# V gathers four places further behind the U gathers in a hybrid mixer and expert-gather kernel

## The reference

```python
q = (xt @ w_query).reshape(T, Hh, 2, PEER_HALF)          # 128 tokens, 8 heads
s = jnp.einsum('thpc,pnc->thpn', q, sub_keys)
sv, si = lax.top_k(s, K)                                 # 16 of 128, twice
fv, fi = lax.top_k(cand, K)                              # 16 of the 256 pair sums
eidx = jnp.take_along_axis(cidx, fi, axis=-1)
g = jax.nn.softmax(fv, axis=-1)
ue, ve = expert_u[eidx], expert_v[eidx]                  # rows of 1024 from 16384 experts
act = jax.nn.gelu(jnp.einsum('td,thkd->thk', xt, ue), approximate=False)
return jnp.einsum('thk,thkd->td', (g * act), ve)
```

## Time and profile before

| | us |
|---|---|
| median of 3 runs | 3545.51 |
| lowest, highest | 3544.26, 3552.44 |
| the profiled execution | 3540.44 |
| its span, first to last instruction | 3538.7 |
| mean granted TensorE clock | 0.765 of full |

### The profile page before, as it was taken

One profiled execution on the slowest core, in us unless ns is written; L12 is line 12 of the kernel. 1 busy time (PEld: TensorE's weight loads), 2 busy tenths in 40 slices (PEclk: granted clock), 3 DMA queues, 4 the chain that ended last, 5 costly groups with the idle time before them and its releaser, 6 DMA issues.

```text
span 3538.7 us, 32708 instructions
## 1 busy us (share of the span) xinstructions
PE 2224.0 (63%) x10776; PEld 1135.5 (32%) x10776; DVE 2182.0 (62%) x5516; ACT 628.7 (18%) x1358; POOL 1941.3 (55%) x2079
## 2 busy tenths in 40 slices
PE   8999986545665466546764478456664577444433
PEld 6767762212322133213421233123321343111110
DVE  4544357765766676666676676657666666665753
ACT  1221132111221022102211132113310232100000
POOL 0000026666666666666666666666466655666665
PEclk9999997776777677767776788677876787766655
DMA  5211369999999999999999999999899999999998
GB/s 193 67 41 38 114 243 360 378 382 361 363 357 392 370 370 343 384 378 360 387 369 376 358 368 354 386 371 349 305 370 377 360 336 346 364 370 377 368 366 325
DMA packets 337953, 1156.72 MB, mean 327 GB/s; under 512 B 36404, under 2 KB 50424, under 8 KB 336760
## 3 DMA queue, kind: packets, MB, share of 16 engines
q0 software_dynamic: 294912, 1073.87, 79.7%
q1 hardware_dynamic: 42872, 80.75, 6.6%
HBM read 1136.64 MB, written 17.84 MB: 326 GB/s over the span
## 4 chain that ended last, share of the span: by engine, by line
PE 30%; POOL 24%; issue 17%; DVE 11%; another core or an unknown queue 10%; DMA 6%; ACT 2%; POOLq 0%; DVEq 0%; ACTq 0%
POOL work L705 12%; POOL work L688 12%; PE xs L1516 10%; PE xs_ahead L1516 8%; PE acc L1516 7%; DVE work L1398 5%; PE bank L1516 4%; DMA work<-expert_u,chosen 4%; DMA work<-expert_v,idx_v 2%; DVE work L1024 1%; DVE cand L1016 1%; DVE rest L1298 0%; DVE work L1016 0%; ACT work L859 0%
## 5 line engine op out<-in xcount | busy, mean ns | idle before, releaser
L1398 DVE CUSTOM_DVE_ANT_0 work<-work,xs 128x1024 f32<-128x1024 f32 x1003 | 1210.7, 1218 | 527.2 <-DMA work<-expert_u,chosen 296.6
L688 POOL DMA_INDIRECT work<-expert_u,chosen x1024 | 966.7, 944 | 859.2 <-DVE chosen L1024 469.6
L705 POOL DMA_INDIRECT work<-expert_v,idx_v x1024 | 969.6, 947 | 720.8 <-remote 316.2
L1516 PE MATMUL acc<-work,lw 128*32 128x512 f32 x4096 | 822.9, 865 | 578.6 <-DMA work<-expert_v,idx_v 303.2
L1516 PEld LDWEIGHTS acc<-work,lw 128*32 128x32 f32 x4096 | 148.2, 138 | 1013.3 <-issue 589.6
L1516 PE MATMUL bank<-weights,n2T 128*128 128x256 f32 x1024 | 255.4, 405 | 0.0
L1516 PEld LDWEIGHTS bank<-weights,n2T 128*128 128x128 f32 x1024 | 203.2, 205 | 110.9 <-issue 84.0
L1516 PE MATMUL bank<-which_eight,c_spread 128*128 128x16 f32 x128 | 35.6, 357 | 309.3 <-issue 143.4
L1516 PE MATMUL xs_ahead<-work,neg_tri 128*128 128x512 f32 (+1 forms) x176 | 130.9, 835 | 129.5 <-DVE work L1024 72.6
L1516 PE MATMUL xs<-work,weights 128*128 128x128 f32 x1664 | 195.4, 280 | 0.0
L1516 PEld LDWEIGHTS xs<-work,weights 128*128 128x128 f32 x1664 | 191.7, 195 | 1.4 <-issue 1.3
(11 more groups left out here) (203 smaller groups left out, 2414.2 us busy)
## 6 DMA issues: line engine op xcount, KB each, us to landing
work<-kv_dram SPq DMA_DIRECT2D x72, 256.0 KB
work<-expert_u,chosen POOLq DMA_INDIRECT x1024
work<-expert_v,idx_v POOLq DMA_INDIRECT x1024
weights<-w_in SPq DMA_DIRECT2D x6, 2048.0 KB, 17.6
mix_dram<-work SPq DMA_DIRECT2D x8, 1024.0 KB, 4.1
weights<-w_queryT SPq DMA_DIRECT2D x4, 2048.0 KB, 7.8
work<-xT SPq DMA_DIRECT2D x9, 512.0 KB, 7.2
kv_dram<-work SPq DMA_DIRECT2D x9, 512.0 KB, 5.9
```

The lines of the kernel that those rows point to most:

```text
L688: pool.indirect_dma_start(out=ring_u[:, s, :], out_offset=None, in_=expert_u, in_offset=bass.IndirectOffsetOnAxis(ap=chosen[:, G % KEPT_HE ...
L705: pool.indirect_dma_start(out=ring_v[:, e % RING_V, :], out_offset=None, in_=expert_v, in_offset=bass.IndirectOffsetOnAxis(ap=idx_v[:, G % ...
L1398: nc.vector.tensor_tensor_reduce(s, s, rows[:, :, :].rearrange("p a b -> p (a b)"), 1.0, 0.0, ALU.mult, ALU.add, dots[:, d:d + 1]).then_in ...
L1516: return nc.tensor.matmul(out_, lhsT, rhs, start=start, stop=stop, skip_group_check=True)
```

## The change

POOL's loop runs over single places instead of heads, and the V gather is the one 20 places (`BEHIND = TOPK + SET`) behind the U gather instead of 16. A head's first V gather is issued with the fifth U gather of the next head instead of the first; at the end 20 V gathers follow the last U gather instead of 16. All other engines' programs, `V_LAG`, both rings and every semaphore value stay.

```diff
+BEHIND = TOPK + SET
...
-            for G in range(HEADS + 1):
+            for n in range(HEADS * TOPK + BEHIND):
+                G, k = divmod(n, TOPK)
                 if G < HEADS:
-                    pool.wait_ge(idx_ready, G + 1)
-                if G > 0:
-                    pool.wait_ge(idx_v_ready, G)
-                for k in range(TOPK):
-                    if G < HEADS:
-                        gather_u(G, k)
-                    if G > 0:
-                        gather_v(G - 1, k)
+                    if k == 0:
+                        pool.wait_ge(idx_ready, G + 1)
+                    gather_u(G, k)
+                G, k = divmod(n - BEHIND, TOPK)
+                if G >= 0:
+                    if k == 0:
+                        pool.wait_ge(idx_v_ready, G + 1)
+                    gather_v(G, k)
```

## The result

The changed kernel takes **3672.61 us** (3665.81 to 3676.30, four runs) against 3544.89 us (3538.02 to 3552.44, four runs) of the kernel before on the same chip: a ratio of **1.0362, 95% interval 1.0332 to 1.0391**, 128 us slower. Forecast were 3580 us and at most 3665 us. The direction was right, the size a bit over a quarter of what came.

A forecast was written before the change was run, and what follows sets the result against it. DMA transfers at nine tenths looked like the bound, with POOL standing about 500 us, 404 us of it before V gathers. Terms 6.6 - 26 + 48 + 6 = +35 us gave 3580 us, 1.0% slower; range 3480 to 3665 us.

The forecast's parts named there:

- (a): Start and end of POOL's gather stream: 20 instead of 16 V gathers after the last U gather, +6.6 us.
- (b): POOL's V gathers waiting for PE: half of 44 stops' recoverable time saved, -26 us, bounds 0 and -123 us.
- held signals: PE's sum done, but word reaches waiting engines late (11.6 us in one head); 119 "remote" V stops, 316.2 us, assumed unchanged.
- (c): PE's scores and mixing queued behind later V sums, delaying DVE: 2 us in 24 heads, +48 us, bounds 0 and +106.
- the cover: U ring's slack before a late dot stops POOL's U gather: 12.5 us in a light head, 1.5 us in a loaded one.
- the prediction's own last sign of being wrong: POOL waiting for dots in heads without mixing would show that the U ring's slack was not there.
- (d): DVE's residual add at place 17 waits for PE's set of place 16: +6 us in all, bounds 0 and 35 us.
- PE's lateness was the bound: Rival, chance 0.28: all 44 V stops for PE vanish and the kernel ends faster, 3435 us, or likelier 3500 us.
- the coupling takes the mixing too: Rival, chance 0.12: z, s and av also late behind PE's sums, 4.4 us in 42 heads; 3737 us, half 3645 us.
- The ends alone: Rival, chance 0.17: transfers fill their engines, stops are only exchanged, nothing but the ends moves; 3545 to 3553 us.

The follow-up runs named there:

- e1: Changed kernel with PE's sums of V sets and the residual add four places later (V_LAG 6): 3602.91 us, 1.0126 to the kernel before.
- e13: The changed kernel, unaltered, on a chip where PE's signals are prompt: 3292.59 us against 3260.93 us for the kernel before, 1.0102.
- e3: Changed kernel with the scores issued on PE ahead of the set's sum at place 4: 3633.10 us, 1.0198 to the kernel before.
- e6: Kernel before with the scores issued on PE ahead of the set's sum at place 4: 3561.68 us, 1.0036.
- e7: Changed kernel; ahead of each U gather POOL also waits for the landing of the one two places earlier: 3845.31 us, 1.0829.
- e9: Changed kernel with at most five gathers in flight (a wait ahead of each V gather), on a chip with prompt signals: 3421.53 us, 1.0491.
- e16: Kernel before with at most five gathers in flight (a wait ahead of each V gather), on a chip with prompt signals: 3406.91 us, 1.0454.
- e12: Kernel before with eight U and nine V buffers instead of 7 and 10, on a chip with prompt signals: 3269.88 us, 1.0024.

## Why the forecast was right in sign and short in size

(a) *The ends* held. The first U gather came at 479.1 us, 3.9 us later than before, which e1 and e13 with the same start don't show (475.7 and 474.9 us) and e3 does (479.0 us), so it belongs to the execution; from the last U gather to the last V gather POOL took 3655.43 - 3624.64 = 30.8 us against 26.3, so +4.4 us for a forecast of 6.6:

```profile
3624.64 0.94 POOL L689 DMA_INDIRECT work<-expert_u,chosen  x1 [0.31 <-issue]
...
3655.43 0.93 POOL L706 DMA_INDIRECT work<-expert_v,idx_v  x1 [0.30 <-issue]
```

(b) *The V gates* were taken at -26 us, with the held signals left where they were. That half failed in fact: the remote stops halved, 316 to 167 us, outside the 60 us given. They lie before the third V gather of a set, and if PE is late or DVE stops the U gathers first, POOL isn't there in time to be stopped. The stops for PE fell to 24.8 us as expected. That the saving would be given back by the U ring was the right idea.

(c) *The coupling* was the right mechanism and the mis-sized term. Three of its parts were measured. The push of the scores was 6.8 us in the head opened above, for 5.6 worked out in a loaded one. In heads without mixing the cover did hold where I had looked: in the sixth head of tile 8 DVE now stands 9.20 us for the scores, more than the 4.6 forecast, and no U gather of that head stops.

```profile
3526.31 4.19 PE L1518 MATMUL bank<-weights,n2T 128*128 128x256 f32 x16
```
```profile
3530.54 0.50 DVE L1296 MAX8 srt<-bank 128x8 f32<-128x128 f32 x2 [9.20 <-PE bank L1518]
```

But in the last three heads of tiles 2 to 7 the U gathers stand 53 us in all where they had stood for none, and in the second head of tile 8, which has no mixing, they stand 12 us (7 behind DVE's wait for scores, 5 behind its wait for the residual add): a cover read off one head was taken for all. That is the prediction's own last sign of being wrong. The step that failed is the sentence that a held signal makes the push cost 0 and that 4.4 us is its upper end. In the second heads, where the signal had mostly been prompt, it is now late by 8 to 11 us, on top of the push; 62 us come from these six heads, against 12 in the sum (2 us each) and 26 at the upper bound. The 24 heads for which the sum had 48 us, at most 106, became 6 x 17.9 = 107 us longer, and that with the saving of (b) already in it. The push also reached DVE by two ways that the sum had at nothing, `weigh` and the mixing: +63 and +91 us of its stops.

(d) *The residual add*: DVE's stops ahead of the eight adds went from 35.3 to 41.5 us, +6.2 for +6. That match is luck: 5.3 us of it are at the last add, behind all gathers (27.3 to 32.6 us), which belongs to the end of (a); the seven adds meant here went from 8.0 to 8.9 us.

Of the rivals, that PE's lateness was the bound is refuted: the V stops went, and nothing was gained. That the coupling takes the mixing too has a number that fits (3645 to 3737 us) and is right in part: DVE's stops in the mixing grew by 91 us, and in the second heads of tiles 6 and 7 they are what held DVE. Its price of 4.4 us in each of 42 heads was not found; the larger part of DVE's growth is that for the scores, 231 us. The ends alone are refuted on both kinds of chip.

What is shown: the exchange of V stops for U stops by way of the work that stands behind PE's wait for V rows (e1), the scores first (e3 with e6), and that where signals are prompt it costs 1.0% (e13). That this is about what the sum had is luck, since the sum was made for a chip with held signals. That the other 96 us or so of the result are the late signals' doing rests on the comparison of chips and on the second heads; it is argued from there and not shown on one chip, for the two kinds of chip differ in their transfers too: the page's 40 slices reach 392 GB/s before the change on the one and 409 GB/s in e13. No version tried beats the kernel before on its own chip.

## What to carry to other kernels

When one queue's work is moved later, list what each consumer has queued behind its wait for it: here the scores did not need the V rows at all, and standing behind them in PE's queue made up 1.6 of the 3.6%. Follow all ways from that wait to the engine that matters: with the scores taken out of it, `weigh` took over much of their stop. A stop removed from an issuing engine is worth only what the other ring can still give, and that has to be read in several heads, the tightest first. And a delay whose cause isn't known, like the held signal, should enter the bounds as a cost on top of a push, not as a cover for it.

## What the runs showed of the hardware

A signal of PE can arrive 8 to 13 us late while POOL issues indirect gathers without a stop, and twice in the kernel before the scores' signal rose 18.8 and 18.5 us after their end (DVE stood for it both times and started within 0.1 us of the rise). In the two traces of the result, signals raised with one to three gathers in flight rose within about 1 us (medians, counted from the start of the raising matmul); with four it was about 3 us before and 5 us after the change, with five about 6 and 8 us. With POOL kept to about four in flight (e7) all were prompt: no signal of scores or sets rose more than 1.8 us after its end. In the profile such a wait is named "remote" or put down to a PE instruction long done. The Trainium skill, page "Perfetto Trace Analysis", section "Tensor Engine Instruction (MATMUL, LD_WEIGHTS)", has the propagation of a semaphore as a step behind the end that the profile reports; it gives no duration, and these runs have 0.01 to 18.8 us from that end to the rise.

It isn't a rule of in-flight gathers alone. In e7 some 50 signals were raised with four in flight and rose in 0.6 us (median), where the unpaced kernels have 3 and 5 us. And on the chips of e9 to e16 eight and more were in flight (e12, e13) and the signals of scores and sets took 0.01 to 0.06 us in the mean. The same program is 8% faster there, 3261 against 3545 us. Whether that is the chip or the time of the run, and what the late signals are queued behind, stays open.
